# Modulation sums shared by VectorE, ScalarE and GpSimd, six pairs of units in three output passes, half products from unit 6, 6, 4 and 4

## The reference, cut to what matters

```python
mod_ctx = (silu_ctx @ w_mod[l] + b_mod[l]).reshape(1, N_MOD, D_MODEL)
mod_lat = (silu_c @ w_mod[l] + b_mod[l]).reshape(-1, N_MOD, D_MODEL)
...
h = rmsnorm(x, ng[0]) * (1.0 + m(1)) + m(0)
x = x + 0.5 * m(2) * rmsnorm(swiglu(h, lw['ffn_wi'][0], lw['ffn_wo'][0]), ng[1])
```

## Time and profile before

| | us |
|---|---|
| median of three runs | 3090.72 |
| profiled execution: span from first to last instruction | 3086.4 |
| what lies around the span (median less span) | 4.3 |
| TensorE busy | 2931.0 (95%) |
| VectorE busy | 2128.5 (69%) |
| ScalarE busy | 1272.3 (41%) |
| GpSimd busy | 415.5 (13%) |

### The profile page before, as it was taken

One profiled execution on the slowest core, in us unless ns is written; L12 is line 12 of the kernel. 1 busy time (PEld: TensorE's weight loads), 2 busy tenths in 40 slices (PEclk: granted clock), 3 DMA queues, 4 the chain that ended last, 5 costly groups with the idle time before them and its releaser, 6 DMA issues.

```text
span 3086.4 us, 62218 instructions
## 1 busy us (share of the span) xinstructions
PE 2931.0 (95%) x26200; PEld 2620.5 (85%) x26200; DVE 2128.5 (69%) x3136; ACT 1272.3 (41%) x2105; POOL 415.5 (13%) x465
## 2 busy tenths in 40 slices
PE   6999999999988899999999999999999889999998
PEld 5999878996777789998789998799877777999986
DVE  3997555766666779974669874657666777687635
ACT  3125454235543441354531454532454435345434
POOL 1000101001333220001100001110023433100100
PEclk8999999999999899999999999999998999999999
DMA  5632334420000236223445123444010004322235
GB/s 227 225 105 95 111 135 150 150 72 27 29 4 13 93 139 227 84 83 130 138 157 190 68 83 137 141 145 155 28 51 7 3 13 159 110 69 83 82 123 171
DMA packets 92915, 325.10 MB, mean 105 GB/s; under 512 B 10288, under 2 KB 13936, under 8 KB 77296
## 3 DMA queue, kind: packets, MB, share of 16 engines
...
HBM read 318.05 MB, written 3.31 MB: 104 GB/s over the span
## 4 chain that ended last, share of the span: by engine, by line
PE 76%; DVE 14%; issue 4%; ACT 3%; DMA 2%; POOL 0%; SPq 0%; ACTq 0%; DVEq 0%; POOLq 0%
PE PS L2573 21%; PE PS L2684 19%; PE PS L2639 17%; PE PS L2583 3%; PE PS L791 2%; PE PS L1563 2%; PE PS L815 1%; PE PS L1542 1%; DMA wo<-in_wo 1%; DVE wo_lo L3092 1%; PE PS L738 1%; PE PS L1555 1%; DVE wi_lo L3076 1%; ACT wo_hi L2801 1%; DMA wm<-in_wm 1%
## 5 line engine op out<-in xcount | busy, mean ns | idle before, releaser
L2573 PE MATMUL PS<-h_hi,wi_hi 128*128 128x384 f32 (+2 forms) x1824 | 453.8, 313 | 24.9 <-DVE wi_lo L3076 14.3
L2573 PE MATMUL PS<-h_hi,wi_lo 128*128 128x384 f32 (+2 forms) x1824 | 450.6, 311 | 0.0
L2573 PE MATMUL PS<-h_lo,wi_hi 128*128 128x384 f32 (+2 forms) x1824 | 450.3, 311 | 0.0
L3092 DVE TENSOR_TENSOR wo_lo<-wo,wo_hi 128x1024 fp32r<-128x1024 f32 x208 | 255.4, 1228 | 257.5 <-ACT wo_hi L2801 256.9
L2684 PE MATMUL PS<-wo_hi,a_hi 128*128 128x512 f32 x968 | 392.7, 406 | 18.4 <-DVE wo_lo L3092 11.8
L2684 PE MATMUL PS<-wo_hi,a_lo 128*128 128x512 f32 x968 | 379.1, 392 | 0.0
L2684 PE MATMUL PS<-wo_lo,a_hi 128*128 128x512 f32 x968 | 378.8, 391 | 0.0
L2801 ACT ACTIVATE wo_hi<-wo 128x1024 fp32r<-128x1024 f32 x208 | 220.2, 1058 | 308.9 <-PE PS L2684 218.4
L2573 PEld LDWEIGHTS PS<-h_hi,wi_hi 128*128 128x128 f32 (+1 forms) x1824 | 294.4, 190 | 30.5 <-DVE wi_lo L3076 16.3
L2573 PEld LDWEIGHTS PS<-h_lo,wi_hi 128*128 128x128 f32 (+1 forms) x1824 | 294.3, 189 | 0.7
L2573 PEld LDWEIGHTS PS<-h_hi,wi_lo 128*128 128x128 f32 (+1 forms) x1824 | 294.3, 190 | 0.7
...
## 6 DMA issues: line engine op xcount, KB each, us to landing
...
wo<-in_wo SPq DMA_DIRECT2D x176, 512.0 KB, 3.2
wm<-in_wm SPq DMA_DIRECT2D x128, 512.0 KB, 5.0
...
wo<-in_wout SPq DMA_DIRECT2D x32, 512.0 KB, 3.2
...
out_y_sample<-x SPq DMA_DIRECT2D x4, 512.0 KB, 5.9
```

Of the source, the lines that this page charges most:

```text
L2573: mm = pe.matmul(PSF[0:cols, at:at + GW[g]], st, h[:, k, GA[g]:GA[g] + GW[g]], start=(k == 0 and q == 0), stop=(k == KD - 1 and q == 2))
L3092: dve.tensor_tensor(wo_lo[:, V % 2, :, :], wo[:, V % 2, :, :], wo_hi[:, V % 2, :, :].bitcast(F32), ALU.subtract).then_inc(s_wol, 1)
```

## The change

Line numbers below 2400 stay near those of before; VectorE's L2399/L2402 become L2433/L2436, L3076 becomes L3170, L3092 becomes L3186, L3100 becomes L3194.

1. FAST is 6, 6, 4, 4: twenty more units are half products (6 + 6 + 6 + 2).
2. VectorE sums column z=0 alone. For column z=1 ScalarE writes a product wm * csil to one of four buffers `prod` (`second_column_products`), and GpSimd adds the products up, seven additions of 128 x 1024 for each pair (`second_column_sums`, L2466).
3. Each VectorE sum now waits for the one just before it (`s_ms` at the running count); before, it waited for the one two earlier.
4. The pairs of units: of the sixteen, two each are summed in input passes 0, 1, 2 and 4 and one each in 3 and 5; two each move to the first half of the output passes 0, 2 and 3, one load, one product and one or two VectorE operations a slot (slots 2 to 18), with buffers of their own.
5. In every input pass VectorE does the first pair's eight sums before `hidden(0)`, and ScalarE its first six products before it empties unit 0. `sum_of(1)` and `sum_of(2)` are built behind units 0 and 1.
6. `cut_wi` of the next pass's unit 1 goes from slot 14 to slot 20 of an FFN's output pass.

```diff
-MOD_SHARES = {0: (MOD_FIRST, 8), 1: (12, 4), 2: (16, 8), 3: (24, 6), 4: (30, 4), 5: (34, 2)}
+MOD_SHARES = {0: (MOD_FIRST, 4), "out0": (8, 4), 1: (12, 4), 2: (16, 4), "out2": (20, 4), 3: (24, 2), "out3": (26, 4),
+              4: (30, 4), 5: (34, 2)}
+IN_PRODUCTS = ((0, 6), (6, KD), (KD, KD + 4), (KD + 4, 2 * KD))
+OUT_PRODUCTS = {b: (b - 2, b - 1) for b in range(2, 2 + 2 * KD)}
-FAST = {0: 12, 2: 12, 3: 10, 5: 6}
+FAST = {0: 6, 2: 6, 3: 4, 5: 4}
...
+        def first_column_sum(dve, k, p, c):
+            ...
+            dve.wait_ge(s_wm[at % MOD_RING], 16 * (at // MOD_RING + 2))
+            ...
+                dve.wait_ge(s_ms, at)
+                a = dve.scalar_tensor_tensor(out=macc[:, 0, :], in0=wm[at % MOD_RING][:], scalar=csil[:, c, 0:1],
+                                             in1=macc[:, 0, :], op0=ALU.mult, op1=ALU.add)
...
+        def second_column_products(act_, k, a, b):
+            ...
+                act_.wait_ge(s_wm[at % MOD_RING], 16 * (at // MOD_RING + 2))
+                if at >= MOD_RING:
+                    p, c = divmod(at - MOD_RING, KD)
+                    act_.wait_ge(s_mp, (KD - 1) * p + max(c, 1))
+                act_.activation(prod[at % MOD_RING][:], wm[at % MOD_RING][:], ACT.Copy,
+                                scale=csil[:, one % KD, 1:2]).then_inc(s_mq, 1)
+        def second_column_sums(pool, k):
+            ...
+                    pool.wait_ge(s_mq, at + 1)
+                    ...
+                    pool.tensor_tensor(macc[:, 1, :], prod[at % MOD_RING][:], before, ALU.add).then_inc(s_mp, 1)
...
                     if at >= MOD_RING:
-                        sp.wait_ge(s_ms, 2 * (at - MOD_RING) + 2)
+                        sp.wait_ge(s_ms, at - MOD_RING + 1)
+                        sp.wait_ge(s_mq, at - MOD_RING + 1)
...
+                    mod_ops(dve, n, 0, KD)
                     for u in range(FAST[n] - 2):
                         hidden(n, u, u % 2)
-                        mod_ops(dve, n, 8 * u, 8 * u + 4)
                         cut_wi(u0(n) + u + 2, u % 2)
-                        mod_ops(dve, n, 8 * u + 4, 8 * u + 8)
+                        if u in IN_MOD["ffn"]:
+                            mod_ops(dve, n, *IN_MOD["ffn"][u])
+                        if u < 2:
+                            sum_of(n, 1 + u)
...
+                    if out_mods(n) and b in OUT_MOD:
+                        if b == 10:
+                            dve.wait_ge(s_ge, 4 * n + 4)
+                        mod_ops(dve, out_mods(n), *OUT_MOD[b])
...
                 h_low_part(n, 3)
+                second_column_sums(pool, n)
...
                 gate_diagonals(n)
+                if out_mods(n):
+                    second_column_sums(pool, out_mods(n))
```

More of the change, by code:

```diff
@@ new lines, in second_column_sums @@
+        def second_column_sums(pool, k):
+            macc, _, _, prod = mod_buffers(k)
+            for p in range(first_pair(k), first_pair(k) + MOD_SHARES[k][1] // 2):
+                for c in range(1, KD):
+                    at = KD * p + c
+                    pool.wait_ge(s_mq, at + 1)
+                    if c == 1:
+                        before = prod[(at - 1) % MOD_RING][:]
+                        if p:
+                            pool.wait_ge(s_mt, 2 * p)
+                    else:
+                        before = macc[:, 1, :]
+                        pool.wait_ge(s_mp, (KD - 1) * p + c - 1)
+                    pool.tensor_tensor(macc[:, 1, :], prod[at % MOD_RING][:], before, ALU.add).then_inc(s_mp, 1)
@@ L2409, in mod_fold @@
+        def mod_fold(dve, k, p, slot, z):
+            macc, _, mred, _ = mod_buffers(k)
+            if z:
+                dve.wait_ge(s_mp, (KD - 1) * (p + 1))
+            else:
+                dve.wait_ge(s_ms, KD * (p + 1))
             if p or z:
@@ L2457, in _, with load_wm @@
                     load_wi(0, 0, 0)
-            def load_wm(n, a, b):
-                for step in range(a, min(b, MOD_SHARES[n][1] // 2 * KD)):
+            def load_wm(n, k, a, b):
+                wm = mod_buffers(k)[1]
+                for step in range(a, min(b, MOD_SHARES[k][1] // 2 * KD)):
                     if step == 0:
-                        if n:
+                        if k != n:
+                            sp.wait_ge(s_in, u0(n) + NF)
+                            sp.wait_ge(s_eb, u0(n) + NF)
+                        elif n:
                             sp.wait_ge(s_om, V0(n))
@@ L2519, in _ @@
                     load_wo(n, b)
+                    if out_mods(n) and b in OUT_LOAD:
+                        load_wm(n, out_mods(n), *OUT_LOAD[b])
             for t in range(NT):
@@ L2939, in step @@
                         silu(U, 0)
+                    second_column_products(act_, n, *IN_PRODUCTS[0])
                     silu(u0(n), 0, n == 0)
                     if n in FAST:
-                        for q in range(1, FAST[n] // 2 - 1):
-                            step(q)
-                        U = u0(n) + FAST[n] - 2
-                        cut_wi(n, FAST[n] - 2, 0)
-                        silu(U - 1, 1)
-                        cut_wi(n, FAST[n] - 1, 1)
+                        for u in range(2, FAST[n]):
+                            cut_wi(n, u, u % 2)
+                            if u - 1 < len(IN_PRODUCTS):
+                                second_column_products(act_, n, *IN_PRODUCTS[u - 1])
+                            if u < FAST[n] - 1:
+                                silu(u0(n) + u - 1, (u - 1) % 2, n == 0 and u == 2)
                         fast_scalar(n)
```

120 lines of the change are left out of this document (81 added, 39 removed).

## The result

The changed kernel takes 3209.51 us (median of four runs, 3207.85 to 3213.16) against 3091.41 for the kernel before on the same chip: 1.039 times as long, with a 95% interval of 1.0373 to 1.0403. The forecast was 3197, +106. The profiled span is 3206.1, which is 119.7 more than before.

The account below looks back on a forecast made before the run. TensorE, busy 95% of the span, was taken to bound the kernel. Terms -35.2 + 50 + 32 + 9 + 8 + 42 = +106 on 3086.4 gave 3192, with 4.3 around the span 3197 us; own range 3145 to 3235, overall 3095 to 3250.

Parts of the forecast that it names:

- Less work on TensorE: FFN input passes: twenty units go from 14.08 to 12.32 us as half products, 35.2 us less.
- Sum and addition in turn: Two-input VectorE sum and GpSimd addition go one after the other, 3.3 us a pair, bounds 1.28 and 3.76.
- Why GpSimd gets in at all: GpSimd slips into the 0.04 us gaps between VectorE's dependent instructions; the new sums have such gaps.
- FFN starts: Unit 2 of four FFN input passes: TensorE stalls 14.5 us instead of 2.1, 12.4 more each, 50 in all.
- Mixer starts: Input passes 1 and 4: a new stall of 14.5 us plus 1.7 of slow clock, 16.2 each, 32 in all.
- Later waits: Input passes 0 and 2: wi_lo of unit 4 comes 2.8 us late, 4.5 with the clock, 9 for both.
- The step into half products: FFN input passes: the step costs 3.3 us now, 2 more in each with VectorE later, 8 in all, bounds 0 and 16.
- Output passes: Output passes 0, 2 and 3: additions and VectorE's work in turn overfill slots 2 to 18, 14 us each, 42 in all.
- a slot of lead: Output passes: the loads, 512 KB a slot more, cost nothing because a slot of lead hides them.
- No contention: Rival: additions run beside the sums, so the kernel gets 21 us faster, 3070 us; chance 0.12.
- GpSimd gives way: Rival: VectorE's sums go through at 1.3 us each and additions crowd later, +19, 3110 us; chance 0.15.
- Each addition in full: Rival: output passes pay every addition, 31 x 3 in place of 42, plus slow clock, +61, 3258 us; chance 0.11.

Follow-up runs that it names:

- experiment 4: The changed kernel with half products starting at units 12, 12, 10 and 6 as before, all else kept: 3245.27 us, ratio 1.0494.
- experiment 8: The changed kernel with each GpSimd addition replaced by a one-input GpSimd multiplication of the same size: 3097.36 us, ratio 1.0017.
- experiment 1: The changed kernel with GpSimd adding only 8 of the 1024 columns, all waits, products and loads kept: 3075.26 us, ratio 0.9942.
- experiment 2: The changed kernel with GpSimd's additions made tiny in the input passes only, whole in the output passes: 3111.66 us, ratio 1.0071.

## Why the prediction was right, point by point

The mechanism came as foretold: a two-input sum and an addition go one after the other, and that makes the loss. That the total is within 12 to 14 us (+106 against +118 by the medians and +119.7 by the spans) is in part luck, since the terms behind the sum miss on both sides and partly cancel, as the points below show. The prediction's own range of 3145 to 3235 also isn't what its bounds give: -17 - 20 and +15 + 8 + 25 round 3197 make 3160 to 3245. The time lies in both.

**Less work on TensorE, -35.2.** Right, as far as two runs tell: 33.9 by the spans, 35.8 by the medians (experiment 4). The units still take 12.31 us, by ScalarE's time line of pass 0:

```profile
237.66 0.44 ACT L2985 ACTIVATE f_s<-PS 128x320 f32<-128x320 f32 x1 [0.71 <-PE PS L2718]
249.97 0.44 ACT L2985 ACTIVATE f_s<-PS 128x320 f32<-128x320 f32 x1 [0.71 <-PE PS L2718]
```

TensorE's busy time fell by only 11.2 us, from 2931.0 to 2919.8: TensorE is busy for 156.9 us at the lower granted clock where it was 106.9. At half the speed these 50 us more cost 25, which is the rest.

**Sum and addition in turn, 3.3 us.** Right, 3.3 in the chain. Of the 112 sums, 71 meet an addition, with a median of 3.24, and 41 don't, with 1.28. Transpositions, reductions and `hidden` keep their length beside an addition (1.25, 1.23, 0.54; 3, 10 and 4 cases), which was assumed. The first sum of a pair, one input too, does not: 1.92 and 2.85 to 2.88 where it meets one, five of sixteen times, and 0.75 alone. The prediction gave it 0.75 everywhere.

**Why GpSimd gets in at all.** Here the reasoning failed, though the number held. It put GpSimd's turn down to the gaps of 0.04 us between dependent sums. In output pass 2 there is no gap. Time lines of DVE and POOL:

```profile
1480.93 3.42 DVE L2436 SCALAR_TENSOR_TENSOR macc_out<-wm_out,csil,macc_out 128x1024 f32<-128x1024 f32 x1
1484.28 3.40 DVE L3186 TENSOR_TENSOR wo_lo<-wo,wo_hi 128x1024 fp32r<-128x1024 f32 x1
1487.60 3.41 DVE L2436 SCALAR_TENSOR_TENSOR macc_out<-wm_out,csil,macc_out 128x1024 f32<-128x1024 f32 x1
```

```profile
1483.41 3.19 POOL L2466 TENSOR_TENSOR macc_out<-prod_out,macc_out 128x1024 f32<-128x1024 f32 x1
```

wo_lo starts 0.07 us before the sum ends, and still the addition that began at 1483.41 goes next and works until 1486.60, wo_lo only after it. Whoever has stood longer goes first. An addition overlaps a sum, a wo_lo or a wi_lo by more than 0.5 us in 150 pairs of rows, and in 147 of them the one that starts first ends first. The three others are first sums of a chain, such as that at 1172.84, that start within 0.01 us of the addition. The diagonals of the earlier trace rows let two instructions pass and don't fit this. They are one-input instructions, like those of experiment 8, which VectorE's work also passed (one took 4.82 us beside wi_lo and a token sum); so one input on GpSimd's side behaves otherwise, and why stays open.

**FFN starts, +12.4 each.** Measured at unit 2: 15.4 us in all four, 13.4 more than the 2.0 of before. The missing microsecond is the rest of two errors. The second of the eight sums, the first with two inputs, was counted as free of the first addition; it took 3.51, 2.3 more with its gap. And wi_lo was counted as waiting for GpSimd's last addition, but that ends before the last sum (1195.16 and 1196.25), so from there to wi_lo's end it is 3.0 us and not 4.3.

**Mixer starts, +16.2 each.** Measured waits of 14.6, and the units' part longer by 15.4 and 19.0, mean 17.2, with a further wait at unit 4 of 5.1 and 5.7 us where idle time was counted on. That this comes near 16.2 is luck: TensorE did stall later in these passes before, at units 7 and 8, for wi_lo and for the modulation's closing matmul (1.9, 1.6 and 1.9 us in pass 1; 0.6, 1.9 and 1.9 in pass 4), and those waits are gone. PE in pass 1:

```profile
582.14 0.69 PE L2652 MATMUL PS<-h_hi,wi_hi 128*128 128x384 f32 x1 [14.64 <-DVE wi_lo L3170]
```

**Later waits, +9.** Too small. Unit 4 waits 5.1 and 5.6 us in passes 0 and 2, where 2.8 were worked out: by the starts of the units, units 3 and 4 of the two passes are 16 us longer. The two token sums were counted as meeting additions, and do (3.69 and 3.57 us in place of 1.49); but wi_lo meets one as well. In 8 of 44 cases it takes 3.6 us in the median and up to 4.41 instead of 2.29. DVE in pass 2, ahead of the wait of 5.63:

```profile
1231.57 3.63 DVE L3170 TENSOR_TENSOR wi_lo<-wi,wi_hi 128x2048 fp32r<-128x2048 f32 x1
```

**The step into half products, +8.** Not there. By the same starts it cost 3.3, 3.3, 3.0 and 2.9 us in passes 0, 2, 3 and 5 before, and costs 1.8, 1.3, 4.4 and 3.6 now, 1 us less in all. So the 6.6 us by which the FFN input passes are above their terms are what is left of larger misses: the starts (units 1 and 2) take 6 more than the 50, the later waits 7 more than the 9, and the first units of passes 0 and 5 some 1.5 each more, with more of their work at the lower granted clock (0.50 for the first 3.4 us of pass 5); the step takes 9 less.

**Output passes, +14 each.** Measured 14.4, 15.1 and 17.3. Without the additions these passes are already 6.4 us longer for the three (experiment 1), so the additions make about 40, and 36 by the medians of experiment 2. Even this was not as foretold in form: the slots don't lengthen evenly to 4.7 to 5.2 us. In output pass 2 ScalarE's wo_hi starts about 4.1 us after the one before in half of the slots and 7.4, 8.2, 8.9 and 11.2 in four of them, a mean of 5.1 over nineteen (97.2 us) against 4.3 before (81.2). The longest comes out of SP's queue. SP's waits in the stretch of these slots (line, what it waited for, us in total, times, the longest):

```profile
SPq L2557 <- DVE wo_lo L3186: 64.9, 17, 6.7
SPq L2544 <- DVE macc_out L2433: 10.6, 2, 10.2
```

And DVE, then ACT, on their time lines:

```profile
1525.31 2.88 DVE L2433 TENSOR_SCALAR macc_out<-wm_out,csil 128x1024 f32<-128x1024 f32 x1
```

```profile
1533.96 1.06 ACT L2884 ACTIVATE wo_hi<-wo 128x1024 fp32r<-128x1024 f32 x1 [8.37 <-DMA wo<-in_wo]
```

SP stood 10.2 us at a weight-tile load until the second pair's first sum, whose turn came late, had read the buffer, and ScalarE stood 8.37 us for the wo load queued behind it. The prediction had costed the loads at nothing, on the ground of a slot of lead; that fails once a sum is late. ScalarE's total wait for wo's transfers shows the size: 115.0 us after, 102.8 in experiment 1.

**The rivals.** "No contention" at 3070 priced itself well: with the additions made narrow the time is 3075. "GpSimd gives way" fails in every start, where the sums stand as long as the additions. "Each addition in full" put 93 us and some 10 of slow clock on the three output passes; measured 46.8.
